# Twenty-eight small float32 products, placed one by one among the large products of a front piece

## The chip, the cores and the metric

The kernel runs on one core of a Trainium2 chip. The metric is the device time in microseconds (us) of one execution. The core has a matrix engine (TensorE, PE in the profile, with its weight loads as PEld), VectorE (DVE), ScalarE (ACT), GpSimd (POOL) and SyncE (SP), which issues most of the transfers (DMAs). Each engine works through its own list of instructions in order. They meet only at semaphores.

## The reference, cut to what matters

One inference step of a one-layer recurrent decoder on 256 prompt tokens and 8 x 8 sample tokens, 320 tokens in all, with a model width of 2048. The input is normalised and multiplied with one combined projection; its columns feed four mixers (RG-LRU, a gated MLP over chunks, RWKV-7, mLSTM) and their gates. Then come a branch product, an output product and a SwiGLU block.

```
hn = _rmsnorm(x, p['norm_pre_mix'])
z = jnp.einsum('btd,dp->btp', hn, p['w_in'])
...
# RG-LRU: block-diagonal gates
r = sigmoid(einsum('btni,nij->btnj', xb, p['lru_wa']) + p['lru_ba'])
i = sigmoid(einsum('btni,nij->btnj', xb, p['lru_wx']) + p['lru_bx'])
...
# RWKV-7: sums over the 64 features of a head, and the output gate
kk = kk / jnp.maximum(jnp.linalg.norm(kk, axis=-1, keepdims=True), 1e-12)
o = _layernorm(o, p['rwkv_ln_g'], p['rwkv_ln_b'], RW_LN_EPS)      # mean and variance over a head
o = o + jnp.sum(r * k * p['rwkv_rk'], axis=-1, keepdims=True) * v
y = o * (jax.nn.sigmoid(gd) @ p['rwkv_g2'])
```

The change concerns seven groups of four small products: the two LRU gates (A_r and A_i), the RWKV sums (C_kk_sum, C_rk_sum, C_mean, C_var) and the RWKV output gate (C_gate).

## The kernel before, in words

All activations lie as 128 features by 320 tokens. A large product is exact to nearly float32 by three products of halves: high weight by high input, high weight by low input, low weight by high input (in the profile lines L1508, L1509, L1510, or L1629 to L1631 where a generator issues them). Its operands are of type float32r.

The weights are streamed in **pieces** of 8 tiles of 128 x 128 (512 KB). The front (the input projection) has 212 pieces, numbered from 0; two of them make one output block of 128 columns. Each piece goes through a ring of four slots: SP loads it (L1723), ACT makes its high half (a copy, L1950), POOL makes its low half in two instructions of 512 columns (L1479), and PE multiplies it: 8 rows of three large products, 24 in all. Then DVE scales the finished block out of its bank (L2128), ACT applies a sigmoid where the block is a gate (L1913) and issues its store (L1915). ACT takes the high half of piece p+3 only when PE has finished piece p-1.

The mixers run beside the front. Their small work for PE is written by hand between pieces in `mixers_pe`: `fill(name, n)` issues n whole pieces and notes the number of the piece reached in `at[name]`; `single` issues one small float32 product of 320 columns (L401) into one of four other banks, and notes `at` for it too. ACT, DVE and SP read these numbers: before a mixer instruction they first do their own part of the front up to the piece noted (`full`, `was_read` and `upto` call it). So `at` sets the order on every other engine. `piece_rows` is a generator that issues a piece row by row, so that small work can be put between rows; before the change only D_num used it, with eight products of 8 columns (L489).

By the kernel's own count A_r stands ahead of piece 26, A_i ahead of 27, C_kk_sum ahead of 121, C_rk_sum ahead of 128, C_mean ahead of 198, and C_var and C_gate ahead of 199. The branch phase (lines L1658 to L1660) starts at piece 212.

Names of the chains: ACT turns the A_r and A_i banks into sigmoids (L818, L821), then takes exponentials, tanh and a root (L826, L829, L833). DVE multiplies (L1002), goes on behind the root (L1006, L1008), scans, and ends with the sum that the product B_sum of the next mixer waits for (L1031, semaphore B_added). For C_kk_sum ACT takes a root of each bank (L911) and DVE makes from them (L1233 to L1241) the input of C_rk_sum, which PE waits for (semaphore C_rk). In the tail of RWKV, DVE normalises (L1372 to L1384), multiplies with C_gate's banks (L1388), makes y_lo (L982) and scales the states (L1394), whose store ACT issues (L928) with a wait, ahead of further weight halves.

Of the kernel before, what the change touches and what calls it, by code (L numbers as in the profile page):

```python
# [96 lines left out]
def build(nc, a):  # L97
# [3 lines left out]
    with ctx:  # L101
        def S(name):

            if name not in sems:
                sems[name] = ctx.enter_context(nc.semaphore(name))
            return sems[name]
# [17 lines left out]
        def K(name, parts=P):  # L124
            at, n = CON[name]
            return con[0:parts, at:at + n]
# [246 lines left out]
        def was_read(eng, *key):  # L373

            if eng in part:
                part[eng](at[key])
            b, i = plan[key]
            eng.wait_ge(S(f"bank_read{b}"), i + 1)

        def mixers_pe(pe, pieces, piece_rows):  # L380

            def fill(name, n):
                at[name] = pieces(n)
# [3 lines left out]
            def bank(*key):  # L387

                at[key] = pieces(0)
                b, i = plan[key]  # L390
                if i:
                    pe.wait_ge(S(f"bank_read{b}"), i)
                return M[b]

            def filled(mm, *key):
                mm.then_inc(S(f"bank_full{plan[key][0]}"), 1)

            def single(lhs, rhs, *key, parts=P):

                o = bank(*key)  # L400
                filled(pe.matmul(o[0:parts, 0:T], lhs, rhs, start=True, stop=True), *key)  # L401
# [3 lines left out]
            pe.wait_ge(S("A_weights_in"), 32)  # L405
            pe.wait_ge(S("A_conv"), 2 * C4)
            pe.wait_ge(S("norm_std"), NORM["x"])
            for c in range(C4):
                single(a_wa[:, c, :], a_xc[:, c, :], "A_r", c)
            fill("A_r_read", 1)  # L410
            for c in range(C4):
                single(a_wx[:, c, :], a_xc[:, c, :], "A_i", c)

            fill("A_tail", 5)

            fill("B_in", 6)
            pe.wait_ge(S("B_added"), 1)
# [34 lines left out]
            for h in range(4):  # L452
# [33 lines left out]
                row = piece_rows()  # L486
# [47 lines left out]

            fill("C_kk", 5)
            pe.wait_ge(S("C_kk_sq"), 1)
            for h in hs:
                single(K("ones2"), c_rk[:, h, :], "C_kk_sum", h)
            fill("C_rk", 7)
            pe.wait_ge(S("C_rk"), 1)  # L540
            for h in hs:
                single(K("ones2"), c_rk[:, h, :], "C_rk_sum", h)
            fill("C_scaled", 14)
            pe.wait_ge(S("C_scaled"), 1)
            for ch in range(5):
                n = ch
# [145 lines left out]

            fill("C_mean", 1)
            was_read(pe, "C_o", 4)
            for h in hs:
                single(K("ones2"), c_t[:, h, :], "C_mean", h)
            fill("C_var", 1)
            pe.wait_ge(S("C_osq"), 1)
            for h in hs:
                single(K("ones2"), c_k[:, h, :], "C_var", h)  # L700
            for h in hs:
                single(c_g2[:, h * P:(h + 1) * P], c_gd, "C_gate", h)

        def padded(sp, dst, samples, name, sem):

            stored(sp, ZB[name] + 3)
            sp.dma_start(dst[:, :, 3:3 + TP], whole(name)[:, :, 0:TP]).then_inc(sem, 16)
            sp.dma_start(samples, whole(name)[:, :, TP:T]).then_inc(sem, 16)
# [784 lines left out]
        def _(pe):  # L1493
# [126 lines left out]
            def piece_rows():  # L1620
# [5 lines left out]
                for k in range(8):  # L1626
# [8 lines left out]
                    yield k  # L1635

            mixers_pe(pe, pieces, piece_rows)
            at["end"] = pieces(END_MORE)
            at["turns"] = pieces((NFRONT - pieces(0)) % 8)
# [853 lines left out]
```

## Time and profile before

| | |
|---|---|
| time, median of 3 runs | 2082.67 us (2082.24 to 2082.75) |
| the profiled execution's own time | 2081.98 us |
| its span in the profile | 2080.2 us |
| PE busy | 2057.8 us, 99% |
| POOL busy | 1455.4 us, 70% |
| ACT busy | 765.3 us, 37% |
| DVE busy | 730.8 us, 35% |
| TensorE clock granted, mean | 0.995 |

A busy engine is one that executes; issuing a DMA and waiting are not counted. Matmuls are pipelined, so their busy times overlap, and the distance from one start to the next says more than the duration of one. One small float32 product leaves two matmul records. A number such as x8 is a count of records.

### The profile page before, as it was taken

The numbers are of one execution on the slowest core, as the hardware profiler recorded it, in microseconds if no ns is written. First come the engines' busy times: TensorE is split into PE (matmuls) and PEld (weight loads), VectorE is DVE, ScalarE is ACT, GpSimd is POOL, SyncE is SP. The second block draws the span as 40 slices with busy tenths as digits, with TensorE's granted clock in tenths as the row PEclk, the third lists the DMA queues.
The fourth block names the chain that finished last, engine by engine and source line by source line (L and its number), as shares of the span: only waits on it lengthen the run. The fifth ranks groups of instructions, "written<-read, shape, count | busy, mean of one in ns | idle before, by whom it ended". The sixth has DMA issues, their size and how long they took to land.

```text
span 2080.2 us, 39888 instructions
## 1 busy us (share of the span) xinstructions
PE 2057.8 (99%) x15931; PEld 2017.6 (97%) x15931; DVE 730.8 (35%) x1118; ACT 765.3 (37%) x939; POOL 1455.4 (70%) x1104
## 2 busy tenths in 40 slices
PE   9999999999999999999999999999999999999997
PEld 8999999999999999999999999999999999999997
DVE  5667644578333323656413511111000111111112
ACT  6354343444422222333335533333333333333332
POOL 7787756569765554678876777777777777777774
PEclk9999999999999999999999999999999999999999
DMA  7655655555544443477643444444444444444542
GB/s 255 208 173 191 197 167 186 187 171 167 165 149 136 137 130 114 131 266 248 225 155 122 153 152 151 142 156 144 151 149 149 149 151 150 149 145 145 154 151 96
DMA packets 124399, 338.90 MB, mean 163 GB/s; under 512 B 14964, under 2 KB 51428, under 8 KB 123912
## 3 DMA queue, kind: packets, MB, share of 16 engines
q1 hardware_dynamic: 106416, 315.73, 47.4%
q10 hardware_dynamic: 17880, 21.70, 2.9%
q8 instruction: 76, 1.25, 0.2%
q14 instruction: 27, 0.22, 0.0%
HBM read 313.50 MB, written 23.89 MB: 162 GB/s over the span
## 4 chain that ended last, share of the span: by engine, by line
PE 55%; POOL 25%; issue 19%; DVE 0%; POOLq 0%; ACT 0%; DVEq 0%
POOL w_lo L1479 25%; PE banks_g L1509 16%; PE banks_g L1510 16%; PE banks_g L1508 16%; PE banks_g L1658 1%; PE banks_m L1658 1%; PE banks_g L1660 1%; PE banks_m L1660 1%; PE banks_g L1659 1%; PE banks_m L1659 1%; PE banks_g L1686 0%; PE banks_g L1687 0%; PE banks_g L1690 0%; PE banks_m L1510 0%; PE banks_m L1509 0%
## 5 line engine op out<-in xcount | busy, mean ns | idle before, releaser
L1479 POOL TENSOR_TENSOR w_lo<-w_raw,w_hi 128x512 fp32r<-128x512 f32 (+1 forms) x1096 | 1449.1, 1347 | 604.5 <-ACT w_hi L1950 283.0
L1508 PE MATMUL banks_g<-x_hi,w_hi 128*128 128x320 f32 x3136 | 983.2, 314 | 0.3 <-ACT arena L880 0.3
L1509 PE MATMUL banks_g<-x_lo,w_hi 128*128 128x320 f32 x3136 | 970.8, 310 | 0.3 <-issue 0.3
L1510 PE MATMUL banks_g<-x_hi,w_lo 128*128 128x320 f32 x3136 | 970.8, 310 | 0.0
L1508 PEld LDWEIGHTS banks_g<-x_hi,w_hi 128*128 128x128 f32 x3136 | 590.3, 188 | 8.2 <-issue 2.4
L1509 PEld LDWEIGHTS banks_g<-x_lo,w_hi 128*128 128x128 f32 x3136 | 590.5, 188 | 2.2 <-issue 0.6
L1510 PEld LDWEIGHTS banks_g<-x_hi,w_lo 128*128 128x128 f32 x3136 | 590.3, 188 | 0.0
L1950 ACT ACTIVATE w_hi<-w_raw 128x1024 fp32r<-128x1024 f32 x196 | 206.1, 1058 | 435.6 <-PE banks_g L1510 376.8
L1831 ACT ACTIVATE w_hi<-w_raw 128x1024 fp32r<-128x1024 f32 (+1 forms) x240 | 249.7, 1041 | 240.3 <-PE banks_g L1510 239.0
L1510 PE MATMUL banks_g<-a_hi,w_lo 128*128 128x320 f32 x704 | 217.5, 309 | 0.0
L1508 PE MATMUL banks_g<-a_hi,w_hi 128*128 128x320 f32 x704 | 217.5, 309 | 0.0
L1509 PE MATMUL banks_g<-a_lo,w_hi 128*128 128x320 f32 x704 | 217.5, 309 | 0.0
L1508 PEld LDWEIGHTS banks_g<-a_hi,w_hi 128*128 128x128 f32 x704 | 132.5, 188 | 0.0
L1509 PEld LDWEIGHTS banks_g<-a_lo,w_hi 128*128 128x128 f32 x704 | 132.5, 188 | 0.0
L1510 PEld LDWEIGHTS banks_g<-a_hi,w_lo 128*128 128x128 f32 x704 | 132.5, 188 | 0.0
L2128 DVE TENSOR_TENSOR ev<-banks_g,rstd 128x320 f32<-128x320 f32 x104 | 49.8, 489 | 231.1 <-PE banks_g L1510 185.9
L2265 DVE TENSOR_TENSOR term<-banks_g,rstd 128x320 f32<-128x320 f32 x40 | 19.7, 492 | 261.9 <-PE banks_g L1510 261.9
L2263 DVE TENSOR_TENSOR gate<-banks_g,rstd 128x320 f32<-128x320 f32 x40 | 19.7, 492 | 188.8 <-PE banks_g L1510 188.8
L2021 ACT ACTIVATE a_hi<-term 128x320 f32 (+1 forms) x44 | 20.7, 470 | 155.7 <-DVE term L2268 148.1
L2057 ACT ACTIVATE w_hi<-w_raw 128x1024 fp32r<-128x1024 f32 (+1 forms) x45 | 44.4, 989 | 89.6 <-PE banks_g L1510 89.6
L2014 ACT ACTIVATE gate<-gate 128x320 f32<-128x320 f32 x41 | 19.4, 473 | 121.3 <-DVE gate L2263 119.2
L1975 ACT ACTIVATE w_hi<-w_raw 128x1024 fp32r<-128x1024 f32 x32 | 34.0, 1061 | 69.6 <-PE banks_m L1660 28.6
(385 smaller groups left out, 1868.5 us busy)
## 6 DMA issues: line engine op xcount, KB each, us to landing
w_raw<-in_w_f SPq DMA_DIRECT2D x211, 512.0 KB, 3.8
w_raw<-in_w_fi SPq DMA_DIRECT2D x176, 512.0 KB, 3.6
w_raw<-in_w_fo SPq DMA_DIRECT2D x64, 512.0 KB, 3.5
front_scratch<-ev ACTq DMA_DIRECT2D x106, 160.0 KB, 2.9
w_raw<-in_w_br SPq DMA_DIRECT2D x32, 512.0 KB, 4.5
w_raw<-in_w_o SPq DMA_DIRECT2D x32, 512.0 KB, 3.6
arena<-front_scratch SPq DMA_DIRECT2D x25, 640.0 KB, 5.6
w_raw<-in_w_fo SPq DMA_DIRECT2D x32, 384.0 KB, 3.0
```

The source lines that it names most:

```text
L1479: low = nc.gpsimd.tensor_tensor(w_lo[:, q % RING, c0:c1], w_raw[:, q % RING, c0:c1], w_hi[:, q % RING, c0:c1].bitcast(F32), ALU.subtract)
L1508: pe.matmul(out, wh, hi[:, k0 + k, :], start=first and k == 0, stop=False)
L1509: pe.matmul(out, wh, lo[:, k0 + k, :], start=False, stop=False)
L1510: mm = pe.matmul(out, wl, hi[:, k0 + k, :], start=False, stop=last and k == tiles - 1)
L1658: pe.matmul(out, wh, y_hi[:, y, :], start=k == 0, stop=False)
L1659: pe.matmul(out, wh, y_lo[:, y, :], start=False, stop=False)
L1660: mm = pe.matmul(out, wl, y_hi[:, y, :], start=False, stop=k == 3)
L1831: nc.scalar.activation(w_hi[:, slot, 0:tiles * P], w_raw[:, slot, 0:tiles * P], ACT.Copy).then_inc(S("w_hi_made"), 1)
L1950: nc.scalar.activation(w_hi[:, q % RING, :], w_raw[:, q % RING, :], ACT.Copy).then_inc(S("w_hi_made"), 1)
L1975: nc.scalar.activation(w_hi[:, q % RING, :], w_raw[:, q % RING, :], ACT.Copy).then_inc(S("w_hi_made"), 1)
L2057: nc.scalar.activation(w_hi[:, p % RING, 0:n], w_raw[:, p % RING, 0:n], ACT.Copy).then_inc(S("w_hi_made"), 1)
L2128: v.tensor_tensor(ev[:, b, :], (G[b] if bank is None else bank)[:, 0:T], rstd[:, :], ALU.mult).then_inc(S(f"evac{b}"), 1)
```

## The change

After each small product two rows of one piece are issued (after each of C_var and C_gate one row), so that a group of four goes with one piece; the eight of C_var and C_gate share one. The whole pieces that a `fill` issues behind are cut by one in three places; A_r_read goes. At C_mean, and at C_var with C_gate, no `fill` is cut, so that each of the two places puts one piece more ahead of `at["end"]`. The number of pieces is the same.

```diff
+            row = piece_rows()
             for c in range(C4):
                 single(a_wa[:, c, :], a_xc[:, c, :], "A_r", c)
-            fill("A_r_read", 1)
+                next(row), next(row)
+            row = piece_rows()
             for c in range(C4):
                 single(a_wx[:, c, :], a_xc[:, c, :], "A_i", c)
-
-            fill("A_tail", 5)
+                next(row), next(row)
+
+            fill("A_tail", 4)
...
+            row = piece_rows()
             for h in hs:
                 single(K("ones2"), c_rk[:, h, :], "C_kk_sum", h)
-            fill("C_rk", 7)
+                next(row), next(row)
+            fill("C_rk", 6)
             pe.wait_ge(S("C_rk"), 1)
+            row = piece_rows()
             for h in hs:
                 single(K("ones2"), c_rk[:, h, :], "C_rk_sum", h)
-            fill("C_scaled", 14)
+                next(row), next(row)
+            fill("C_scaled", 13)
...
             was_read(pe, "C_o", 4)
+            row = piece_rows()
             for h in hs:
                 single(K("ones2"), c_t[:, h, :], "C_mean", h)
+                next(row), next(row)
             fill("C_var", 1)
             pe.wait_ge(S("C_osq"), 1)
+            row = piece_rows()
             for h in hs:
                 single(K("ones2"), c_k[:, h, :], "C_var", h)
+                next(row)
             for h in hs:
                 single(c_g2[:, h * P:(h + 1) * P], c_gd, "C_gate", h)
+                next(row)
```

On PE at A_r, before (banks_g takes the large products, banks_m the small ones):

```order
L1510 MATMUL banks_g<-x_hi,w_lo 128x320
L401 MATMUL banks_m<-arena 128x320 x4
L1508 MATMUL banks_g<-x_hi,w_hi 128x320
L1509 MATMUL banks_g<-x_lo,w_hi 128x320
L1510 MATMUL banks_g<-x_hi,w_lo 128x320
```

and now, at the same place (L1522 is L1510 of before; L1641 to L1643 are the generator's three products):

```order
L1522 MATMUL banks_g<-x_hi,w_lo 128x320
L401 MATMUL banks_m<-arena 128x320
L1641 MATMUL banks_g<-x_hi,w_hi 128x320
L1642 MATMUL banks_g<-x_lo,w_hi 128x320
L1643 MATMUL banks_g<-x_hi,w_lo 128x320
L1641 MATMUL banks_g<-x_hi,w_hi 128x320
L1642 MATMUL banks_g<-x_lo,w_hi 128x320
L1643 MATMUL banks_g<-x_hi,w_lo 128x320
L401 MATMUL banks_m<-arena 128x320
```

The second, third and fourth small product of the group now stand 6, 12 and 18 large products later. The first stays.

On ACT in the tail of RWKV, before (L919 reads C_var's banks, L924 makes y_hi, L926 and L928 store the states, L1950 makes high halves of weights):

```order
L919 ACTIVATE arena<-banks_m,vec 128x320 x4
L1950 ACTIVATE w_hi<-w_raw 128x1024 x2
L1913 ACT_TABLE_LOAD
...
L924 ACTIVATE y_hi<-arena 128x320 x4
L926 DMA out_Sp<-arena 128x256
L928 DMA out_Ss<-arena 128x2048
L1950 ACTIVATE w_hi<-w_raw 128x1024 x2
L1913 ACTIVATE ev<-ev 128x320
L1915 DMA front_scratch<-ev 128x320
L1950 ACTIVATE w_hi<-w_raw 128x1024 x2
```

and now (L931, L936, L938 and L940 are L919, L924, L926 and L928 of before, L1962 is L1950, L1925 and L1927 are L1913 and L1915):

```order
L931 ACTIVATE arena<-banks_m,vec 128x320 x4
L1962 ACTIVATE w_hi<-w_raw 128x1024 x3
L1925 ACT_TABLE_LOAD
...
L936 ACTIVATE y_hi<-arena 128x320 x4
L938 DMA out_Sp<-arena 128x256
L940 DMA out_Ss<-arena 128x2048
L1962 ACTIVATE w_hi<-w_raw 128x1024 x2
L1925 ACTIVATE ev<-ev 128x320
L1927 DMA front_scratch<-ev 128x320
L1962 ACTIVATE w_hi<-w_raw 128x1024
```

Two high halves of weights have moved from behind the waiting store L928 to ahead of it: they are now those of pieces 210 and 211, and the first behind it is that of piece 212.

## Rows read from the trace of the kernel before

**Rows 1.** Page, parts 1 and 2: busy time, and the granted clock in slices

```profile
PE 2057.8 (99%) x15931; PEld 2017.6 (97%) x15931; DVE 730.8 (35%) x1118; ACT 765.3 (37%) x939; POOL 1455.4 (70%) x1104
PEclk9999999999999999999999999999999999999999
```

**Rows 2.** Waits of PE: total us, times, longest

```profile
PE banks_m L427 <- DVE arena L1047: 3.0, 1, 3.0
PE banks_g L1658 <- POOL w_lo L1479: 1.1, 1, 1.1
```

**Rows 3.** Timeline of PE at A_r (start us, length, operation, records)

```profile
102.43 2.31 PE L401 MATMUL banks_m<-arena 128*128 128x320 f32 x8
104.34 0.55 PE L1508 MATMUL banks_g<-x_hi,w_hi 128*128 128x320 f32 x1
104.73 0.31 PE L1509 MATMUL banks_g<-x_lo,w_hi 128*128 128x320 f32 x1
104.88 0.31 PE L1510 MATMUL banks_g<-x_hi,w_lo 128*128 128x320 f32 x1
```

**Rows 4.** Timeline of PE at B_sum, a small product alone

```profile
148.97 0.70 PE L401 MATMUL banks_m<-arena,con 128*128 128x320 f32 x2
149.26 0.55 PE L1508 MATMUL banks_g<-x_hi,w_hi 128*128 128x320 f32 x1
149.65 0.31 PE L1509 MATMUL banks_g<-x_lo,w_hi 128*128 128x320 f32 x1
```

**Rows 5.** Timeline of PE in D_num, a product of 8 columns between rows

```profile
290.94 0.31 PE L1630 MATMUL banks_g<-x_lo,w_hi 128*128 128x320 f32 x1
...
291.62 0.31 PE L1630 MATMUL banks_g<-x_lo,w_hi 128*128 128x320 f32 x1
```

**Rows 6.** Timeline of ACT at A_i

```profile
108.84 2.14 ACT L821 ACTIVATE arena<-banks_m,vec 128x320 f32<-128x320 f32 x4 [1.68 <-PE banks_m L401]
```

**Rows 7.** Timeline of DVE behind A_i, to B_sum's input and its next wait

```profile
111.11 1.49 DVE L1002 TENSOR_TENSOR arena<-arena 128x1280 f32<-128x1280 f32 x1 [7.99 <-ACT arena L821]
120.55 1.49 DVE L1006 SCALAR_TENSOR_TENSOR arena<-arena 128x1280 f32<-128x1280 f32 x1 [6.10 <-ACT arena L833]
144.77 1.47 DVE L1031 TENSOR_TENSOR arena<-arena 128x320 f32<-128x320 f32 x1
149.22 0.49 DVE L2128 TENSOR_TENSOR ev<-banks_g,rstd 128x320 f32<-128x320 f32 x1 [2.98 <-PE banks_g L1510]
```

**Rows 8.** Timeline of POOL: the two low halves of piece 32

```profile
121.55 4.17 POOL L1479 TENSOR_TENSOR w_lo<-w_raw,w_hi 128x512 fp32r<-128x512 f32 x2 [0.99 <-ACT w_hi L1950]
```

**Rows 9.** Timeline of PE: first product of piece 32

```profile
127.84 0.31 PE L1508 MATMUL banks_g<-x_hi,w_hi 128*128 128x320 f32 x1
```

**Rows 10.** Timelines of ACT and DVE from C_kk_sum to C_rk

```profile
501.13 2.05 ACT L911 ACTIVATE arena<-banks_m 128x320 f32<-128x320 f32 x4 [0.91 <-PE banks_m L401]
522.43 2.48 DVE L1241 TENSOR_TENSOR arena<-arena,vec 128x1280 f32<-128x1280 f32 x1
```

**Rows 11.** Timeline of PE at C_rk_sum

```profile
527.18 1.24 PE L401 MATMUL banks_m<-arena,con 128*128 128x320 f32 x4
```

**Rows 12.** Timelines of DVE, ACT, POOL and PE at the end of the mixers

```profile
847.90 2.30 DVE L1375 TENSOR_TENSOR arena<-arena 128x1280 f32<-128x1280 f32 x1
850.59 2.31 PE L401 MATMUL banks_m<-arena,con 128*128 128x320 f32 x8
882.23 3.82 DVE L982 TENSOR_TENSOR y_lo<-arena,y_hi 128x320 fp32r<-128x320 f32 x4 [0.35 <-ACT y_hi L924]
888.93 2.01 ACT L1950 ACTIVATE w_hi<-w_raw 128x1024 fp32r<-128x1024 f32 x2 [5.75 <-DVE arena L1394]
890.08 3.82 POOL L1479 TENSOR_TENSOR w_lo<-w_raw,w_hi 128x512 fp32r<-128x512 f32 x3 [5.18 <-ACT w_hi L1950]
893.62 0.31 PE L1508 MATMUL banks_g<-x_hi,w_hi 128*128 128x320 f32 x1
```

**Rows 13.** Window behind the wait of L427: busy us of PE, PEld, DVE, ACT, POOL, then clock

```profile
171.90:175.30 3.40, 3.40 (x16) 3.26 (x15) 0.00 (x0) 3.09 (x5) 0.17 (x1) 0.52 0.63 185
```

## The prediction

> **What bounds the kernel now.** I read the page first. PE is busy for 2057.8 of 2080.2 us and the granted clock is full in every slice [rows 1]: the time is the sum of PE's distances from one start to the next, plus its waits. The list of waits comes next: the longest is 3.0 us at L427, and near the seven groups of the change there is none; at the start of the branch phase stands one of 1.1 us for the low halves [rows 2]. So the change can act in two ways only: a small product may cost PE more or less in its new place, or a result that comes later may turn a margin into a wait. The timelines of PE at the groups price the first, those of ACT, DVE and POOL behind them the second.
>
> **Cost of a small product on PE.** In the row of four, the group begins at 102.43, and the second large product behind it starts at 104.73. A large product follows its neighbour by 0.15 us (104.73 to 104.88) [rows 3]. I measure to the second large product because the first is recorded early. The four cost 104.73 - 102.43 - 0.15 = 2.15 us, 0.54 each. A small product alone between large ones goes from 148.97 to 149.65, less 0.15: 0.53 [rows 4]. Twenty-eight products of 0.54 us are 15 us in the row and 15 us alone, so the term is 0. The operation to be bounded is this product in the middle of a piece, which the trace shows only with 8 columns: a row of three large products with one such product takes 291.62 - 290.94 = 0.68 us [rows 5], against 0.44 without, so 0.24 us for an insertion with almost no columns. If that were a price of switching that comes on top in mid-piece, the 21 further insertions (28 instead of 7) would cost 21 x 0.24 = 5.0 us. From below, if both records of a small product followed like large ones, each would take 0.29 us, 28 x 0.25 = 7.0 us less. I take 0: rows 4 have the same columns and the same switch on both sides.
>
> The Trainium skill (TensorE: Matmul & The Clock Gate, Step-by-step: what each phase is for) says that the engine pulls a weight load ahead of the matmul in flight, so that one tile's weights load while another's columns stream. Read for this change, a small product behind a large one would hide a load that a neighbour in the row cannot, and the change would gain; with rows 4 at the price of rows 3, the gain by that reading is put at nothing here, and it stays as a rival.
>
> **The results that come later.** A group starts where it did, but its fourth product has 18 large products ahead of it: 18 x 0.147 = 2.6 us later. The group and its piece together take PE the same time, so all behind them on PE stays put until there is a wait.
>
> *A_r.* ACT's four sigmoids end up to 2.6 us later, still ahead of A_i, and one weight half waits behind them. I put this at 0: two whole pieces of 3.5 us are between that half and its use.
>
> *A_i.* ACT's last sigmoid ends at 108.84 + 2.14 = 110.98 [rows 6] and DVE starts at 111.11; that becomes 113.7. ACT works through to the root without idling, so DVE goes on at 123.2 in place of 120.55, and ends B_sum's input at 148.9 in place of 146.24 [rows 7]. PE wants to load for B_sum at 148.82, its product being at 148.97 [rows 4]: 0.1 us late. DVE's chain ends its lag there, since its next step waited 2.98 us for PE [rows 7]. Queued behind ACT's exponentials and root are the high halves of pieces 30 to 33. For piece 32 POOL starts at 121.55 and ends at 125.72, and PE begins the piece at 127.84 [rows 8, 9]: a margin of 2.1 against a lag of 2.6 is a wait of 0.5 us. It covers B_sum's 0.1. Bounds: 0 where POOL takes the 2.55 us for a piece that it takes beside an idle DVE (3.82 for three halves in [rows 12]) instead of 4.17; above, 0.5 plus the same 1.6 once more on a neighbouring piece, 2.1 us. I take 0.6.
>
> *The later wait of 3.0 us at L427* does not absorb this: its chain starts at B_sum, which moves with PE.
>
> *C_kk_sum.* ACT's roots end at 503.18 now and 505.8 then. DVE's chain behind them has no idle time up to L1241, which ends at 524.91 [rows 10] and then at 527.5. PE loads for C_rk_sum at 527.03, its product being at 527.18 [rows 11]: a wait of 0.5 us, and 0.1 for a product that starts out of a wait. Bounds: 0 if one 1280-element step takes 1.49 us as in [rows 7] and not 2.48; above, one step more at that difference, 1.6 us. I take 0.6. Behind the waiting product PE holds back the front for as long; ACT and POOL are ahead by more.
>
> *C_rk_sum.* Its readers wait for a piece, not for it: 0.
>
> *C_mean, C_var, C_gate.* C_mean's fourth comes 2.6 us later, so the square L1375 ends at 850.20 + 2.6 = 852.8 [rows 12]. C_var's place, at 850.59 before [rows 12], is one piece further on, at 854.1: no wait. Each C_gate needs its bank read by ACT; it comes 3.9 us behind C_var of the same bank and had 2.2 before: no wait. What moves is the end of the mixers. `at["end"]` is two pieces later (209 for 207), 2 x 3.52 = 7.0 us. y_lo ends at 886.05 + 7.0 = 893.1 [rows 12], and the branch phase needs it at piece 212, which starts at 893.62 + 2 x 3.52 = 900.7 (893.62 is the start of piece 210 in [rows 12]): cover of 7.6 us. The first weight half behind the waiting store goes from 888.93 to 896.0. Before, it was that of piece 210: POOL started at 890.08 and needed 2.55, ready at 892.6 for 893.62, a margin of 1.0 [rows 12]. Now it is that of piece 212: ready at 899.7 for 900.7, the same margin. ACT's last stores, on which the 1.1 us wait of the branch phase hangs, come some 0.1 us later. I take 0.1; bounds 0 and 1.1, a doubled wait.
>
> **Sum.** 0 + 0.6 + 0.6 + 0.1 = 1.3 us on the profiled execution's own 2081.98 gives 2083.3. That execution is 0.7 below the median of the runs, 2082.67. On the runs' scale I forecast 2084.0 us. What a measurement of this kernel can tell from no change is 0.2%, 4.2 us.
>
> **Rivals.**
>
> 1. *The margins hold.* POOL meets DVE otherwise once all is shifted, and both waits stay at nothing: 2082.7 us. For it: the shortfalls are only 0.5 us of 2.6. Against it: two places at once.
> 2. *A switch costs more in mid-piece*, 5.0 us by the bound above, with the waits 6.3: 2089.0 us, slower. For it: 0.24 us for 8 columns [rows 5]. Against: the single product in rows 4 pays no more than its share in rows 3.
> 3. *POOL falls behind, and the clock with it*, slower. Place: pieces 30 to 43, beside DVE's long chain. After the wait for L427 TensorE's clock was at 0.52, which is the level of 1.2 GHz, for 3.4 us [rows 13]; it cost 1.6 us of work. Were the whole lag of 2.6 us and POOL's 1.6 to come together as one wait of 4.2, as long as that one, with 1.6 us of clock: 5.8, with the other 0.7 it is 6.5, 2089.2 us. It decides where the wait comes to that one's 3.0 us; I expect 0.5.
> 4. *The cost in the row is hidden by the neighbours*, 7.0 us less, with the waits 5.7 less: 2077.0 us, faster.
>
> On rival 3 the Trainium skill (SBUF — State Buffer) has a rule that speaks against the change: a GpSimd instruction and a VectorE instruction with two inputs from SBUF take the shared port pair as an exclusive lock, and the other fully blocks. By that rule each half on POOL may wait for a whole DVE instruction, and the 4.17 us of piece 32 would come again on the pieces behind. The trace agrees in kind: 4.17 us beside DVE, 2.55 beside an idle one.
>
> **How the numbers follow.** Forecast 0.68, rival 1 0.22, rival 2 0.03, rival 3 0.04, rival 4 0.03. Faster by over 0.2% is rival 4, 0.03; slower by over 0.2% rivals 2 and 3, 0.07; within 0.2% the rest, 0.90. The forecast's own bounds are 0 to 4.8 us (2.1 + 1.6 + 1.1), 2082.7 to 2087.5; all three upper ends together are unlikely, so I set the upper end at 2086.5. Below, rival 1 with the spread of the runs (0.4 us) gives 2082.2.
>
> **What would show it.** In the timeline of the changed kernel: 0.54 us for each small product, measured as above, in mid-piece (right) or 0.7 and more (rival 2) or 0.3 (rival 4). In the list of PE's waits: a new one of about 0.5 us for POOL at piece 32 (start at 128.4 and not 127.84), one of about 0.6 us at C_rk_sum for DVE L1241's successor, and that of the branch phase at 1.1 to 1.3. A wait of over 2 us anywhere, or a second window at the clock's lower level ahead of piece 100, would make the forecast wrong. So would a wait at C_gate or at y_lo.

## The result and the profile after

| | before | changed |
|---|---|---|
| median of 20 runs each, taken side by side | 2081.86 us (2079.17 to 2082.94) | 2084.96 us (2083.43 to 2085.92) |
| profiled execution's own time | 2081.98 us | 2084.93 us |
| span | 2080.2 us | 2083.1 us |

The ratio is 1.0016, with a 95% interval of 1.0010 to 1.0023: 3.3 us more by the ratio and 3.1 us between the medians, inside the 0.2% that was called no change, and 1.0 us over the forecast of 2084.0. The loss is real, since the interval excludes 1, and it is larger than the 1.3 us of the sum. So most of this part asks where the rest was lost.

The page of the changed kernel, parts 1 and 2, answers to [rows 1]:

```profile
PE 2055.4 (99%) x15931; PEld 2015.1 (97%) x15931; DVE 728.9 (35%) x1118; ACT 764.9 (37%) x939; POOL 1454.6 (70%) x1104
PEclk9999999999999999999999999999999999999999
```

PE is 2.4 us less busy in a span 2.9 us longer: what was added is waiting. (Not all of the 5.3 us more of idle time is loss: in a stretch at the lower clock the same products count as busy for longer, and the changed kernel has less of such stretches, as shown below.) The list of PE's waits (total us, times, longest) answers to [rows 2]:

```profile
PE banks_m L430 <- DVE arena L1059: 5.0, 1, 5.0
PE banks_g L1670 <- POOL w_lo L1491: 1.3, 1, 1.3
```

L430 is L427 of before, L1670 is L1658. The second wait went from 1.1 to 1.3 us, as forecast. The first is the one of which the prediction said that it does not take part, and it went from 3.0 to 5.0 us.

Small products in the middle of a piece, in the timeline of PE at A_r ([rows 3] before):

```profile
104.19 0.70 PE L401 MATMUL banks_m<-arena 128*128 128x320 f32 x2
104.48 0.55 PE L1641 MATMUL banks_g<-x_hi,w_hi 128*128 128x320 f32 x1
104.87 0.31 PE L1642 MATMUL banks_g<-x_lo,w_hi 128*128 128x320 f32 x1
105.61 0.70 PE L401 MATMUL banks_m<-arena 128*128 128x320 f32 x2
```

From one small product to the next are 105.61 - 104.19 = 1.42 us, with six large ones of 0.147 between: the small one takes 0.54 us. All 28 lie between 0.535 and 0.543 us.

Piece 32, in the timelines of POOL and PE ([rows 8, 9] before):

```profile
124.53 5.42 POOL L1491 TENSOR_TENSOR w_lo<-w_raw,w_hi 128x512 fp32r<-128x512 f32 x3 [0.97 <-ACT w_hi L1962]
```
```profile
128.84 0.38 PE L1520 MATMUL banks_g<-x_hi,w_hi 128*128 128x320 f32 x1 [0.48 <-POOL w_lo L1491]
```

POOL starts 2.98 us later than the 121.55 of before, takes 4.17 us for the two halves of piece 32 again (to 128.70; the third record is a half of the next piece), and PE, which was due at 128.21, waits for 0.48 us. This is the term of 0.5 us. PE's start at 128.84 is later than the forecast 128.4, mostly since the whole trace already stood 0.34 us later at start-up, before the first changed instruction.

C_kk_sum and C_rk, in the timelines of ACT, DVE and PE ([rows 10, 11] before):

```profile
509.55 0.44 ACT L923 ACTIVATE arena<-banks_m 128x320 f32<-128x320 f32 x1 [0.98 <-PE banks_m L401]
```
```profile
510.12 0.83 DVE L1245 TENSOR_SCALAR arena<-arena 128x1280 f32<-128x1280 f32 x1 [8.38 <-ACT arena L923]
528.87 1.49 DVE L1253 TENSOR_TENSOR arena<-arena,vec 128x1280 f32<-128x1280 f32 x1
```
```profile
531.34 0.70 PE L401 MATMUL banks_m<-arena,con 128*128 128x320 f32 x2
```

The roots end 2.6 us later against PE, as forecast, but DVE's last step takes 1.49 us and not the 2.48 of [rows 10]; the chain ends at 530.36, 0.8 us ahead of PE's load for the product at 531.34, and PE does not wait.

**The wait at L427.** The product at L427 turns mixer B's normalised rows over (a transposition). It rests on B_var, the sum behind the variance, a single product at L401 that PE issued at 156.64 us. The expectations below call this wait the one at B_var's product, or that for L1047 (L1059 in the changed kernel), DVE's last step ahead of it. The prediction had no rows for what ends it. Here is the chain behind it, before, on SP, ACT, DVE and PE (start us, length, operation, records, idle time and what ended it; SPq and ACTq are issues of DMAs):

```profile
137.40 5.50 DVE L982 TENSOR_TENSOR y_lo<-arena,y_hi 128x320 fp32r<-128x320 f32 x4
142.82 0.87 DVE L2128 TENSOR_TENSOR ev<-banks_g,rstd 128x320 f32<-128x320 f32 x2
```
```profile
143.33 0.35 ACTq L1915 DMA_DIRECT2D front_scratch<-ev  x1
158.39 1.06 ACT L1950 ACTIVATE w_hi<-w_raw 128x1024 fp32r<-128x1024 f32 x1 [6.58 <-DMA w_raw<-in_w_f]
160.76 0.53 ACT L848 ACTIVATE arena<-banks_m,vec 128x320 f32<-128x320 f32 x1
```
```profile
150.06 0.33 SPq L744 DMA_DIRECT2D arena<-front_scratch  x1
154.06 1.38 SPq L1723 DMA_DIRECT2D w_raw<-in_w_f  x3
```

In the list of SP's own waits (total us, times, longest):

```profile
SPq L744 <- DMA front_scratch<-ev: 6.2, 1, 6.2
```

Then DVE and PE:

```profile
161.32 2.15 DVE L1044 RECIPROCAL arena<-arena 128x320 f32<-128x320 f32 x1 [2.33 <-ACT arena L848]
```
```profile
170.99 2.13 PE L427 MATMUL banks_m<-con,arena 128*128 128x128 f32 x12 [2.99 <-DVE arena L1047]
```

And after:

```profile
145.79 0.87 DVE L2140 TENSOR_TENSOR ev<-banks_g,rstd 128x320 f32<-128x320 f32 x2
```
```profile
146.29 0.35 ACTq L1927 DMA_DIRECT2D front_scratch<-ev  x1
161.76 1.06 ACT L1962 ACTIVATE w_hi<-w_raw 128x1024 fp32r<-128x1024 f32 x1 [6.94 <-DMA w_raw<-in_w_f]
164.13 0.53 ACT L860 ACTIVATE arena<-banks_m,vec 128x320 f32<-128x320 f32 x1
```
```profile
153.57 0.33 SPq L756 DMA_DIRECT2D arena<-front_scratch  x1
157.57 0.43 SPq L1735 DMA_DIRECT2D w_raw<-in_w_f  x1
```
```profile
164.69 2.15 DVE L1056 RECIPROCAL arena<-arena 128x320 f32<-128x320 f32 x1 [4.03 <-ACT arena L860]
```
```profile
174.33 1.97 PE L430 MATMUL banks_m<-con,arena 128*128 128x128 f32 x8 [4.98 <-DVE arena L1059]
```

Read it backwards. PE waits for DVE's four products, which stand behind a reciprocal; the reciprocal waited for ACT's root of B_var. The root stands on ACT behind the high half of piece 42, and ACT stood idle there until that piece's weights had landed. SP had issued their load (the first L1723 behind L744) behind nine transfers for the next mixer, of which L744 is the first, and L744 waits for the store of a front block (6.2 us in the list). DVE scales that block out of its bank behind its y_lo of mixer A. So DVE's A chain, which A_i's lag moves, reaches the root over a store and a load; B_sum is not on the way. Each link stands 3.0 to 3.5 us later: 142.82 to 145.79, 143.33 to 146.29, 150.06 to 153.57, 154.06 to 157.57, 158.39 to 161.76, 160.76 to 164.13.

**Where the 2.95 us between the two profiled executions went.** To the start of the product at L427 the changed kernel loses 174.33 - 170.99 = 3.34 us: 0.34 at start-up, 0.53 at piece 32 and B_var together (the wait of 0.48 and a slower start out of it cost 0.7; 0.2 comes back at B_var, whose input came 0.2 us late before and is in time now), 0.48 at piece 42 and 2.0 of the longer wait. Piece 42 was in time before. Now its high half, which comes late with its weights, makes its low half late too, in the timelines of POOL and PE:

```profile
162.90 2.55 POOL L1491 TENSOR_TENSOR w_lo<-w_raw,w_hi 128x512 fp32r<-128x512 f32 x2 [2.91 <-ACT w_hi L1962]
```
```profile
165.60 0.39 PE L1520 MATMUL banks_g<-x_hi,w_hi 128*128 128x320 f32 x1 [0.25 <-POOL w_lo L1491]
```

Then the clock. In windows of before (us, busy us of PE, PEld, DVE, ACT, POOL, then granted clock) TensorE is at half of full, the level of 1.2 GHz, behind the wait, and again at two places where neither kernel's order differs:

```profile
171.78:175.18 3.40, 3.40 (x16) 3.26 (x15) 0.00 (x0) 3.09 (x5) 0.29 (x1) 0.50 0.63 187
813.48:820.28 6.80, 6.80 (x51) 6.68 (x48) 0.42 (x1) 0.00 (x0) 0.33 (x1) 0.50 0.25 80
1130.92:1134.32 3.40, 3.01 (x12) 2.64 (x12) 3.33 (x9) 1.71 (x4) 1.76 (x2) 0.50 0.13 26
```

and after:

```profile
172.72:179.52 6.80, 5.19 (x22) 5.05 (x23) 1.95 (x3) 3.50 (x5) 2.69 (x2) 0.50 0.62 198
817.84:821.24 3.40, 3.40 (x35) 3.28 (x33) 0.42 (x1) 0.00 (x0) 0.21 (x1) 0.50 0.51 153
```

Behind the wait the changed kernel runs more of its work at the lower level, and PE's records fall back by 0.8 us more; at 813 to 821 it runs less there and gets 1.5 us back. With 0.2 us at the branch phase and small rest this makes 2.95 us. The stretch at 1130 us costs the kernel before nothing: from the product at L1523 (L1535 now) just ahead of it to PE's last one pass 940.3 us in both profiles.

### The profile page after: what moved, and what is told of

It is laid out like the page before. It is cut to its first block, busy times and chain, and to the rows that moved or that the text cites. A ratio compares the mean times of both kernels' runs of the same rounds, so it can differ in the third digit from the quotient of the medians.

```text
span 2083.1 us, 39888 instructions
## 1 busy us (share of the span) xinstructions
PE 2055.4 (99%) x15931; PEld 2015.1 (97%) x15931; DVE 728.9 (35%) x1118; ACT 764.9 (37%) x939; POOL 1454.6 (70%) x1104
## 4 chain that ended last, share of the span: by engine, by line
PE 54%; POOL 24%; issue 19%; DVE 1%; ACT 1%; POOLq 0%; DVEq 0%
POOL w_lo L1491 24%; PE banks_g L1521 16%; PE banks_g L1522 16%; PE banks_g L1520 16%; PE banks_g L1670 1%; PE banks_g L1672 1%; PE banks_m L1672 1%; PE banks_m L1671 1%; PE banks_g L1671 1%; PE banks_m L1670 1%; DVE banks_m L2240 0%; DVE banks_m L2214 0%; ACT x_hi L2015 0%; POOLq L1485 0%; POOLq L1489 0%
## 5 line engine op out<-in xcount | busy, mean ns | idle before, releaser
L1520 PE MATMUL banks_g<-x_hi,w_hi 128*128 128x320 f32 x3088 | 966.2, 313 | 1.0 <-POOL w_lo L1491 0.7
L1521 PE MATMUL banks_g<-x_lo,w_hi 128*128 128x320 f32 x3088 | 954.9, 309 | 0.4 <-issue 0.4
L1522 PE MATMUL banks_g<-x_hi,w_lo 128*128 128x320 f32 x3088 | 955.0, 309 | 0.0
L1520 PEld LDWEIGHTS banks_g<-x_hi,w_hi 128*128 128x128 f32 x3088 | 580.5, 188 | 8.9 <-issue 3.6
L1521 PEld LDWEIGHTS banks_g<-x_lo,w_hi 128*128 128x128 f32 x3088 | 580.8, 188 | 1.8 <-issue 0.7
L1522 PEld LDWEIGHTS banks_g<-x_hi,w_lo 128*128 128x128 f32 x3088 | 580.5, 188 | 0.0
L1962 ACT ACTIVATE w_hi<-w_raw 128x1024 fp32r<-128x1024 f32 x196 | 205.6, 1057 | 429.0 <-PE banks_g L1522 358.7
L1522 PE MATMUL banks_g<-a_hi,w_lo 128*128 128x320 f32 x704 | 217.4, 309 | 0.0
L1522 PEld LDWEIGHTS banks_g<-a_hi,w_lo 128*128 128x128 f32 x704 | 132.4, 188 | 0.0
```

Source lines behind the costliest of these rows:

```text
L1520: pe.matmul(out, wh, hi[:, k0 + k, :], start=first and k == 0, stop=False)
L1521: pe.matmul(out, wh, lo[:, k0 + k, :], start=False, stop=False)
L1522: mm = pe.matmul(out, wl, hi[:, k0 + k, :], start=False, stop=last and k == tiles - 1)
L1962: nc.scalar.activation(w_hi[:, q % RING, :], w_raw[:, q % RING, :], ACT.Copy).then_inc(S("w_hi_made"), 1)
```

## The experiments

Each kernel below was run 11 times (before_both 9) with 25 to 33 runs of the kernel before beside it on the same chip, whose medians were 2082.26 to 2082.47 us. Single runs of one kernel spread over 3 to 7.5 us, so the starts of the product at L427 in the profiled executions are given beside the medians.

**1. Which part costs: a_only, c_only, ai_only.** Each takes over a part of the diff and leaves the rest as before. a_only takes the hunk of A_r and A_i from the diff shown ahead, and c_only all the others. ai_only's edit is this:

```diff
             for c in range(C4):
                 single(a_wa[:, c, :], a_xc[:, c, :], "A_r", c)
             fill("A_r_read", 1)
+            row = piece_rows()
             for c in range(C4):
                 single(a_wx[:, c, :], a_xc[:, c, :], "A_i", c)
-
-            fill("A_tail", 5)
+                next(row), next(row)
+            fill("A_tail", 4)
```

> The LRU gates A_r and A_i placed singly as in the changed kernel, the RWKV products four in a row as before. Theory 1 (the lag of A_i's last product, 18 x 0.147 = 2.6 us, runs on through DVE's y_lo, SP's weight loads and ACT's wait for them to the root of B_var, and comes out at the wait for L1047, which grows from 3.3 to 5.3 us between matmul starts; piece 32 waits 0.5 us for its low half): all of the loss is here, 2.5 to 3.5 us over before, wait at L1047 about 5.2 us. Theory 2 (the loss is spread over the seven groups, as my forecast had it, half at A and half at C_rk): 1.2 to 1.6 us over before, and the wait at L1047 grows only by chance.

> The 20 RWKV products placed singly, the LRU gates as before. Theory 1: no loss, within 0.4 us of before; wait for L1047 at 3.0 to 3.3 us as before; no wait at C_rk_sum. Theory 2: 0.6 to 1.6 us over before with a wait at C_rk_sum or at the start of the branch phase.

> Only A_i's four products placed singly (A_r and all RWKV groups as before). Theory 1: A_r's lag is caught up ahead of A_i and costs nothing, so the time is that of the kernel with both LRU gates singly, 2.5 to 3.5 us over before. Rival (A_r's lag adds, through ACT's later weight half): at least 1 us less than that kernel.

| kernel | median us | ratio, 95% interval | L427's product starts |
|---|---|---|---|
| a_only | 2085.51 | 1.0013 [1.0004, 1.0022] | 174.98 |
| ai_only | 2085.64 | 1.0012 [1.0002, 1.0021] | 173.40 |
| c_only | 2082.63 | 0.9998 [0.9989, 1.0008] | 172.52 |

A_i's four products carry the loss; A_r adds nothing to it that these runs can tell, and the twenty products of mixer C cost 0.3 us between the medians, with an interval from -2.3 to +1.7 us. Theory 1 had all of this. It did not have the wait of c_only, which it put at 3.0 to 3.3 us. Up to 300 us behind B_var it issues the instructions of before, and yet its profile shows the wait at 4.8 us and not 3.0:

```profile
159.94 1.06 ACT L1959 ACTIVATE w_hi<-w_raw 128x1024 fp32r<-128x1024 f32 x1 [7.32 <-DMA w_raw<-in_w_f]
```
```profile
172.52 2.82 PE L427 MATMUL banks_m<-con,arena 128*128 128x128 f32 x12 [4.83 <-DVE arena L1056]
```

The same link, piece 42's load, landed 1.5 us later. So the length of that wait differs between executions by nearly as much as the change moves it, and one pair of profiles can't price it. The start of the product is the better mark: 170.99 and 172.52 without A_i's lag; 173.40, 174.12, 174.33 and 174.98 with it (174.12 is after_sp_wait, below). The means differ by 2.5 us.

**2. Half the lag: ai_one_row.** One row behind each product of A_i, and the other four behind the group, so that the fourth is 1.3 us later and not 2.6.

```diff
             for c in range(C4):
                 single(a_wx[:, c, :], a_xc[:, c, :], "A_i", c)
-                next(row), next(row)
+                next(row)
+            for _ in range(4):
+                next(row)
```

> The changed kernel with A_i alone changed, and by half the dose: one row of a piece behind each of A_i's four products, the other four rows of that piece behind the group. The fourth product then comes 9 x 0.147 = 1.3 us later instead of 2.6. Theory (the lag of the A chain travels past PE over DVE, a store and the loads to the high half of piece 42, and lengthens the wait at B_var's product): the root ahead of B_var comes 1.3 us later instead of 2.6 to 3.4, that wait grows by 1.0 to 1.5 us, piece 32 has its low halves in time (its shortfall of 0.5 us goes), and the time is 1.0 to 2.0 us over the kernel before. Rival (the wait at B_var varies by itself between 3 and 5 us and the loss of the A_i kernel is something that comes with any row between its products): the loss stays at the 2.5 to 3.4 us that the full dose gave.

Measured: 2084.11 us beside 2082.47, ratio 1.0008 [0.9999, 1.0017], against 1.0012 to 1.0013 for the full lag. ACT's root starts at 162.19 us, which is 1.4 later than in before's profile and 1.9 earlier than in the changed kernel's; the product follows at 172.40:

```profile
162.19 0.53 ACT L852 ACTIVATE arena<-banks_m,vec 128x320 f32<-128x320 f32 x1
```
```profile
172.40 2.82 PE L431 MATMUL banks_m<-con,arena 128*128 128x128 f32 x12 [4.61 <-DVE arena L1051]
```

The loss of 1.6 us is the theory's (1.0 to 2.0) and half of what A_i's full lag costs, and piece 32 does not wait, as it said. But the interval goes from none to 3.5 us, and c_only, without any lag ahead of this wait, has the root at 162.31 and the product at 172.52, no earlier than here. So this run fits the theory and does not decide against the rival.

**3. The first link tried, which was wrong: after_sp_wait.** In the changed kernel SP's wait for y_lo stands ahead of the loads of pieces 40 and 41. Here it comes behind them.

```diff
             after("A_tail")
-            sp.wait_ge(S("y_lo_made"), C4)
             low = zD[ZB["low"]]
             stored(sp, ZB["low"])
+            sp.wait_ge(S("y_lo_made"), C4)
```

> The changed kernel, but SP issues its weight loads of pieces 40 and 41 before it waits for y_lo, and not behind that wait. If SP's wait is the link that carries the lag (theory 1), the loads are issued 1 to 3 us earlier, B_var's root comes earlier, and the wait for L1059 shrinks from 5.3 to 2.5 to 4 us: 1.5 to 3 us under the changed kernel, about the time of before. If the lag travels on DVE and ACT alone (rival), nothing moves: within 0.4 us of the changed kernel.

Measured: 2085.27 us beside 2082.29, ratio 1.0016 [1.0007, 1.0025], as the changed kernel. SP issues the two loads at 144.16 and not at 145.89:

```profile
144.16 1.12 SPq L1735 DMA_DIRECT2D w_raw<-in_w_f  x2
153.26 0.33 SPq L756 DMA_DIRECT2D arena<-front_scratch  x1
157.47 2.39 SPq L1735 DMA_DIRECT2D w_raw<-in_w_f  x4
```

but the first weights land at the same time (the high half behind them starts at 152.03 in both), L756 goes at 153.26 in place of 153.57, and the wait stays 5.0 us. An issue 1.7 us earlier gained nothing. The reading is that the loads stood behind the transfers of mixer B that SP had issued just ahead; after_ws below, where three of these go earlier, has that high half at 149.42. The link over y_lo's wait is refuted: the time is the rival's, within 0.4 us of the changed kernel.

**4. Cutting the link, in both kernels: before_ahead and after_ahead.** The loads of pieces 42 and 43 go ahead of the nine transfers of the next mixer. SP's wait for y_lo goes behind them too, which alone changed nothing in the changed kernel (after_sp_wait).

```diff
             after("A_tail")
-            sp.wait_ge(S("y_lo_made"), C4)
             low = zD[ZB["low"]]
+            part[sp](2 * ZB["low"] + 5 + AFTER + 2)
             stored(sp, ZB["low"])
+            sp.wait_ge(S("y_lo_made"), C4)
```

> The kernel before, with SP's weight loads of pieces 42 and 43 issued ahead of the nine small mixer transfers instead of behind them. Theory (B_var's root stands on ACT behind the high half of piece 42, which waits for its weights, and so sets the 3 to 5 us wait of PE at L1047): piece 42's weights land near 152 to 154 us and not at 158 to 160, the root starts about 2 us earlier, bound then by B_var itself, and PE's wait shrinks by 2 us or more: 2 to 4 us faster than before, the clock's fall behind the wait included. Rival (the wait is DVE's own work from B_sum on): same as before within 0.5 us.

> The changed kernel with the same two loads ahead of the mixer transfers, and SP's wait for y_lo behind them. Theory: the link between A_i's lag and B_var's root is cut, since the root then follows B_var and not the weights; PE's wait at L1059 falls from 5.0 to 1 to 3 us, and the kernel comes to within 1.5 us of the kernel before with the same loads, 2080 to 2082 us. Rival (the lag of A_i reaches the wait over DVE): the gap of 3 us between changed and unchanged stays.

**5. A gain that leaves the link: before_ws and after_ws.** The three constants of mixer B are loaded ahead of the wait for gv's store; piece 42's load stays where it was.

```diff
+            sp.dma_start(b_ws, a["ws"]).then_inc(S("B_ws_in"), 16)
+            sp.dma_start(b_wss, a["wss"]).then_inc(S("B_ws_in"), 16)
+            sp.dma_start(b_bias, a["gbias"].broadcast_to([P, C4, T])).then_inc(S("B_ws_in"), 16)
             stored(sp, ZB["gv"] + 3)
...
             sp.dma_start(b_u, whole("gu")).then_inc(S("B_u_in"), 16)
-            sp.dma_start(b_ws, a["ws"]).then_inc(S("B_ws_in"), 16)
-            sp.dma_start(b_wss, a["wss"]).then_inc(S("B_ws_in"), 16)
-            sp.dma_start(b_bias, a["gbias"].broadcast_to([P, C4, T])).then_inc(S("B_ws_in"), 16)
```

> The kernel before, with the three constant transfers of the gated MLP (weights and bias, 1.2 MB) issued ahead of SP's wait for block gv's store instead of behind the load of gu. Theory (the weights of pieces 40 and 41 stand in the queue behind them): these weights land 2 to 4 us earlier than 149.4 us, but piece 42's weights still come behind the mixer transfers, so the wait at L1047 shrinks by 1 to 3 us: 1 to 3 us faster. Rival: they only take bandwidth elsewhere: same.

> The changed kernel with the three constant transfers early. Theory: the loss against the kernel before shrinks from 3.2 us to 0.5 to 2 us, since the queue no longer adds 1.2 MB behind the late load of gu; piece 32's wait of 0.5 us stays. Rival: 3 us over before as the changed kernel.

**6. Both shifts together: before_both and after_both.**

> The kernel before with both shifts of loads: the three constants of the B mixer ahead of the wait for gv's store, and the loads of pieces 42 and 43 ahead of the nine transfers of the next mixer. Theory (the wait at B_var's product ends with the root, which stands behind the high half of piece 42; that half waits for its load): both together take the half's weights away as the last to come, the wait is bounded by PE and the DVE reciprocal, 1.5 to 2.5 us, and the time is 1.8 to 2.8 us under the kernel before. Rival (each shift gains by something of its own): the two gains add, 2.3 + 1.8 = 4.1 us.

> The changed kernel with both shifts of loads. Theory: as for the unchanged kernel with both, wait at B_var's product 1.5 to 2.5 us, time 1.8 to 3.8 us under the kernel before, and within 1.5 us of the unchanged kernel with both shifts, since the lag has no way to B_var any more except by DVE's own chain, which PE's order covers. Rival (the change has a cost of its own beside this wait): 3 us over the unchanged kernel with both shifts.

| pair | before's order: ratio; start; wait | changed order: ratio; start; wait | starts apart |
|---|---|---|---|
| no shift | (1); 170.99, 172.52; 3.0, 4.8 | 1.0016 [1.0010, 1.0023]; 174.33; 5.0 | +2.6 |
| ws | 0.9988 [0.9979, 0.9997]; 169.98; 1.9 | 1.0004 [0.9995, 1.0013]; 171.67; 3.3 | +1.7 |
| ahead | 0.9992 [0.9983, 1.0001]; 170.58; 2.5 | 0.9989 [0.9980, 0.9998]; 170.12; 1.5 | -0.5 |
| both | 0.9976 [0.9966, 0.9986]; 169.98; 1.0 | 0.9995 [0.9986, 1.0004]; 171.43; 2.8 | +1.5 |

A cell has the ratio to the kernel before, the start of the product at L427 and PE's wait ahead of it. Without a shift, before's order has two starts and two waits, of before and of c_only, and the difference is to the mean of the two. The medians, in order: 2079.93 and 2082.57 us for ws, 2080.44 and 2078.46 for ahead, 2077.97 and 2081.80 for both.

In after_ahead the wait fell from 5.0 to 1.5 us and the loss is gone: its ratio to before lies under 1, and its median 2.0 us under that of before_ahead, where the changed order had been 3.1 us over. Piece 42's high half now comes at 155.94 and not 161.76, and the root follows it:

```profile
155.94 1.06 ACT L1963 ACTIVATE w_hi<-w_raw 128x1024 fp32r<-128x1024 f32 x1 [0.28 <-DMA w_raw<-in_w_f]
158.31 0.53 ACT L861 ACTIVATE arena<-banks_m,vec 128x320 f32<-128x320 f32 x1
```
```profile
170.12 1.53 PE L430 MATMUL banks_m<-con,arena 128*128 128x128 f32 x12 [1.50 <-DVE arena L1060]
```

In before_ahead the two come at 153.60 and 157.60, and the root there waits for B_var on PE:

```profile
153.60 1.06 ACT L1951 ACTIVATE w_hi<-w_raw 128x1024 fp32r<-128x1024 f32 x1 [0.54 <-PE banks_g L1511]
157.60 0.53 ACT L849 ACTIVATE arena<-banks_m,vec 128x320 f32<-128x320 f32 x1 [1.64 <-PE banks_m L401]
```

Piece 32 waits for 0.47 us in after_ahead too. With the loads ahead DVE no longer idles for the root in either kernel: it is DVE's own chain from B_sum on that the product then waits for. So the load of piece 42 carried the lag to the root. That the changed order now starts 0.5 us earlier is in part luck: one step of DVE's chain (128 x 640) took 0.82 us in its profile and 1.80 in that of before_ahead.

The expectations came out so. before_ahead gained 1.8 us (interval from 3.5 less to 0.2 more) and its wait 0.5, under the 2 to 4 and the 2 or more expected, since DVE's own work ends the wait there, as its rival says. after_ahead's wait is in its range, its time 1.5 us below it. before_ws is in its ranges (2.3 us, wait 1.9). after_ws, at 0.3 us over before, is below its 0.5 to 2, and its interval, up to 2.7 us, leaves out its rival of 3. In the ws pair, where it is left in, both kernels gain and the changed one stays behind.

The third pair does not fit. With both shifts the root starts at 158.48 in before_both and 158.16 in after_both, so the lag no longer reaches it, and yet the changed order is slower. The difference is in DVE's own steps to the product:

```profile
159.18 0.41 DVE L1043 TENSOR_TENSOR arena<-arena,con 64x256 f32<-64x256 f32 x1
162.09 1.85 DVE L1046 TENSOR_TENSOR arena<-arena 128x1280 f32<-128x1280 f32 x1
```

in before_both, and in after_both:

```profile
158.87 1.52 DVE L1055 TENSOR_TENSOR arena<-arena,con 64x256 f32<-64x256 f32 x1
162.88 2.54 DVE L1058 TENSOR_TENSOR arena<-arena 128x1280 f32<-128x1280 f32 x1
```

Two steps are longer by 1.1 and 0.7 us, one earlier step is 0.7 shorter, and DVE's chain begins 0.3 later: together the 1.5 us at the product. What the first step takes goes with POOL: in the four profiles where POOL is idle during it (before, before_ws, after_ws, before_both) it takes 0.41 us, in the nine where POOL works beside it 1.50 to 1.52. So the changed order can also cost by where DVE's steps fall against POOL's. Of the 3.4 us between these two profiled executions, 1.5 stand at the product, and 1.7 come from the clock: the stretch at its lower level at 812 us is 6.8 us long in after_both and 3.4 in before_both. Whether the change causes either in every execution is not shown and stays open.

The expectation that both shifts would bring the two orders within 1.5 us failed (3.8 us), and so did after_both's time (0.7 us under before for 1.8 to 3.8) and wait (2.8 for 1.5 to 2.5): its rival, a cost of the change beside this link, holds here. before_both gained 4.5 us where 1.8 to 2.8 were expected. That is nearer to its rival, by which the gains add: 0.9988 times 0.9992 is 0.9980, and 0.9976 was measured. before_both is the best version found, 0.24% [0.14%, 0.34%] under the kernel before, in the order of before and not in the changed one.

**What follows the product.** Two lines mark a place just ahead of the stretch at 1130 us, before and now:

```profile
1127.31 0.72 PE L1523 MATMUL banks_m<-con,ssum 128*128 128x1 f32 x6
```
```profile
1130.26 0.72 PE L1535 MATMUL banks_m<-con,ssum 128*128 128x1 f32 x6
```

From the start of the product at L427 to there pass 1127.31 - 170.99 = 956.3 us before and 1130.26 - 174.33 = 955.9 now. Take off half of the time that PE was busy at the clock's lower level in between (5.1 and 4.3 us) and it is 951.2 and 951.6; over all thirteen profiles 951.2 to 952.4. From there to PE's last product it is 940.3 to 941.0 us in all, with the stretch at 1130 or without it. Behind the product at L427, then, the profiles differ by 1.2 us and 0.7 us at most, whatever the order of the small products; what differs more is the clock. How often TensorE falls to the lower level at 813 us and at 1130 us differs between profiles: 6.8 and 3.4 us in before, 3.4 and none in the changed kernel, none at either place in after_ahead. (Ahead of the stretch at 813 PE was busy without a gap, at the end with 128 records of 8 columns.) The stretch at 813 moves single executions by up to 3.3 us: in the three profiles without a fall behind the wait and with 0, 3.4 and 6.8 us of it (after_ahead, before_both, after_both) the way from L427 to the mark takes 952.0, 953.4 and 955.3 us.

So a rival had to be asked: could the loss be one of the clock? Each run's mean granted clock is on record in steps of 0.001. At 0.995 the ten runs of a_only, ai_only and after_sp_wait take 2085.2 us in the mean, and the eighteen of before beside them 2082.7; at 0.997 it is 2082.7 (ten runs) and 2079.7 (one). The loss stands at equal clock. So does the cut: with the loads ahead the changed order is 0.6 to 1.0 us faster at 0.995, 0.996 and 0.997, so that half or more of its 2.0 us is clock. And so does the third pair: with both shifts the changed order is 2.3 us slower at 0.996 (four runs each), for 3.8 between the medians.

## Why the prediction was right, and where it was not

The forecast (2084.0 us, most likely "within 0.2%") held with its range. Its sum did not: it had 1.3 us, and the runs show 3.1 to 3.3. By its own signs it was wrong as well: no wait of over 2 us was to come, and that at L427 grew by 2.0 to 5.0 us; and ahead of piece 100 the stretch at the clock's lower level became twice as long.

- *A small product costs 0.54 us in a piece as in the row*: right, 0.535 to 0.543 us for all 28. Rivals 2 (a dearer switch) and 4 (a hidden cost) fall with it, and c_only's 0.9998 agrees in run time.
- *A_r at 0*: right; ai_only and a_only cost the same.
- *A_i, 0.6 us at piece 32 for POOL*: right: 0.47 or 0.48 us in all seven profiles with the full lag, and no wait there in ai_one_row and c_only. Not foreseen was the 0.48 us at piece 42, which comes from the late load of the next point and not from POOL's own work.
- *"The later wait of 3.0 us at L427 does not absorb this: its chain starts at B_sum, which moves with PE"*: this is the step that failed. The chain ends over ACT's root, which stands behind a weight half, whose load SP holds behind a transfer that waits for a store that DVE's A chain holds back. The lag of 2.6 us went round PE on this way and arrived in the wait: 2.0 us there, 0.5 more at piece 42, some 2.5 us of the start over all profiles, and up to 0.8 us of slower clock behind it. The prediction asked who the wait's releaser waits for on PE, and did not follow it through the queues; the reciprocal's idle time of 2.33 us, ended by ACT and not by PE, stood in the trace of before.
- *C_rk_sum, 0.6 us*: wrong. The lag came (2.6 us), but DVE's chain became 1.4 us shorter (L1253 1.49 us for 2.48, L1245 0.83 for 1.16), which left 0.8 us of cover ahead of PE's load. The lower bound, 0 for one step at 1.49 us, was the truth; the error was to take the durations of steps beside POOL as fixed under a shift.
- *C_mean, C_var, C_gate and the end of the mixers, 0.1 us*: right; no wait at C_gate or at y_lo, and 1.3 us at the branch phase. y_lo ends at 895.76 and the first high half behind the store starts at 898.64, where 893.1 and 896.0 were forecast and the whole trace stood 2.7 us later.
- *Rival 3* named stage and sum about right, pieces 30 to 43 and the clock, with one wait that grows there by the lag; it put it on POOL, and it was a load on ACT. It should have had more than 0.04. The rule that it takes from the Trainium skill (SBUF — State Buffer), that of a GpSimd and a two-input VectorE instruction one fully blocks the other, is not what decided: the two halves of piece 32 took 4.17 us again, and the pieces ahead of it 2.56.

So two terms of 0.6 us were forecast, of which one came, and one of 2 to 3 us was missing. That the time still lay in the range is owed to a wide upper end.

## What to carry to other kernels

A wait that is already there is the first place to look for what a later result will cost: follow its chain back through every queue, to the load that ended an engine's idle time, to the transfer that this load stood behind, and to the store that this one waited for, until it comes to something that the change moves. An engine other than the bottleneck that issues stores, or works ahead of them, passes a lag on by way of DMAs, past the engine whose order looks unchanged. And where a wait's length comes from a load's landing, compare several executions before pricing it by one pair.

## What the runs showed of the hardware

- A float32 product of 320 columns costs TensorE 0.54 us whether its neighbours are of its own kind or float32r products of 0.147 us (0.535 to 0.543 for all 28).
- The landing of a load of the same program at the same place differed by 1.5 us between two executions (high half of piece 42 at 158.39 and 159.94), and the wait behind it was 3.0 and 4.8 us.
- Loads issued 1.7 us earlier behind other transfers of the same queue landed no earlier (144.16 for 145.89; the high half behind them at 152.03 in both).
- One VectorE step of 64 x 256 with two inputs took 0.41 us where GpSimd was idle (four profiles) and 1.50 to 1.52 us where it worked beside (nine).
- After a wait of 1.9 to 5.0 us TensorE's clock fell to the level of 1.2 GHz in nine of the thirteen profiles, for 3.4 or 6.8 us; after those of 1.0 and 1.5 it did not, nor after 2.8 (after_both) and 3.3 (after_ws). So the length of the wait alone doesn't tell it.
- A stretch of 3.4 us at 1.2 GHz cost 1.3 us at 813 us (953.4 for 952.0), where TensorE is busy throughout, and 0 to 0.7 us at 1130 us, where TensorE waits for other engines as well.
